# The recurrent unit's steps placed between seven-product tiles, ahead of the attention

## The reference, cut to what matters

```
h = rms_norm_2(x, g_pre) * (1 + scale) + shift
proj = h @ w_in                       # 1024 x 9216 columns
q, k, v, g_att, u, g_lru, merge = split(proj)
y_a = (dilated_attention(q, k, v) * silu(g_att)) @ w_pa
u = causal_depthwise_conv(u, conv_w, conv_b)          # 4 taps
y_b = (rg_lru(u, ...) * silu(g_lru)) @ w_pb
out = (sigmoid(merge)_a * y_a + sigmoid(merge)_b * y_b) @ w_o

rg_lru: r, i = sigmoid(block-diagonal products of u with w_rg, w_ig + biases)
        a = exp(-8 r softplus(-lambda));  h_t = a_t h_(t-1) + sqrt(1 - a_t^2) (i_t u_t)
```

## Time and profile before

| | |
|---|---|
| median of three runs | 2789.05 us |
| the profiled execution | 2786.48 us, of which its span is 2784.7 us |
| PE busy | 2733.2 us, 98% of the span |
| DVE, ACT, POOL busy | 2000.1, 1558.0, 301.9 us |
| stretch of the 18 sets | 1753.67 to 2096.48 us from the span's start |
| stretch of the recurrent unit | 2344.88 to about 2533 us |

### The profile page before, as it was taken

The page is one execution under the profiler, slowest core; times in us unless marked ns, Lnnn a source line. Parts: engine busy times, 40 slices in busy tenths (PEclk is TensorE's granted clock), DMA queues, the critical chain, the costliest instruction groups (busy, mean ns, idle before and its releaser), DMA issues.

```text
span 2784.7 us, 33128 instructions
## 1 busy us (share of the span) xinstructions
PE 2733.2 (98%) x13148; PEld 2280.7 (82%) x13148; DVE 2000.1 (72%) x2300; ACT 1558.0 (56%) x1724; POOL 301.9 (11%) x179
## 2 busy tenths in 40 slices
PE   8999999969999999999999998999999999999999
PEld 7888788858888888888888887888888888888887
DVE  7554457778888888888888888755555565666664
ACT  5322322247777777777777776322335666997122
POOL 0211000020000000000000001332321111112000
PEclk9999999989999999999999999999999999999999
DMA  6222248689999999999999964243333443114442
GB/s 198 95 75 65 87 153 291 247 344 375 385 385 386 387 386 386 386 384 390 384 386 384 386 228 164 95 121 111 101 121 134 129 122 102 49 48 144 169 149 91
DMA packets 181546, 628.30 MB, mean 226 GB/s; under 512 B 43920, under 2 KB 78096, under 8 KB 125840
## 3 DMA queue, kind: packets, MB, share of 16 engines
q1 hardware_dynamic: 176496, 609.46, 58.8%
q0 software_dynamic: 4464, 16.25, 2.2%
q10 hardware_dynamic: 432, 0.47, 0.1%
HBM read 557.74 MB, written 67.21 MB: 224 GB/s over the span
## 4 chain that ended last, share of the span: by engine, by line
PE 95%; DVE 3%; ACT 1%; DMA 1%; issue 0%; SPq 0%; DVEq 0%; ACTq 0%
PE bank L468 25%; PE bank L470 25%; PE bank L469 25%; PE bank L1894 13%; PE bank L476 3%; PE bank L2801 1%; PE bank L485 1%; PE bank L1443 1%; PE bank L794 1%; PE bank L3299 0%; DVE r_sc L1677 0%; DVE r_at L1678 0%; DVE r_best L1674 0%; PE bank L2802 0%; PE bank L854 0%
## 5 line engine op out<-in xcount | busy, mean ns | idle before, releaser
L1842 DVE TENSOR_TENSOR e_wl<-e_raw,e_wh 128x2048 fp32r<-128x2048 f32 x381 | 870.8, 2291 | 123.9 <-ACT e_wh L1834 123.5
L1834 ACT ACTIVATE e_wh<-e_raw 128x2048 fp32r<-128x2048 f32 x384 | 735.7, 1919 | 184.4 <-PE bank L470 101.0
L468 PE MATMUL bank<-e_wh,e_xh 128*128 128x512 f32 x1020 | 403.4, 395 | 0.0
L470 PE MATMUL bank<-e_wh,e_xl 128*128 128x512 f32 x1020 | 398.1, 390 | 0.0
L469 PE MATMUL bank<-e_wl,e_xh 128*128 128x512 f32 x1020 | 396.9, 389 | 0.0
L470 PEld LDWEIGHTS bank<-e_wh,e_xl 128*128 128x128 f32 x1020 | 191.4, 188 | 41.0
L469 PEld LDWEIGHTS bank<-e_wl,e_xh 128*128 128x128 f32 x1020 | 191.8, 188 | 38.1
L468 PEld LDWEIGHTS bank<-e_wh,e_xh 128*128 128x128 f32 x1020 | 191.6, 188 | 38.0 <-DVE e_wl L1842 0.4
L1894 PE MATMUL bank<-e_wh,e_hh 128*128 128x512 f32 x512 | 159.1, 392 | 0.0
L1894 PE MATMUL bank<-e_wl,e_hh 128*128 128x512 f32 x512 | 157.8, 389 | 0.0
L1894 PE MATMUL bank<-e_wh,e_hl 128*128 128x512 f32 x512 | 157.8, 389 | 0.0
(11 more groups left out here) (579 smaller groups left out, 5864.3 us busy)
## 6 DMA issues: line engine op xcount, KB each, us to landing
e_raw<-in_e_gate_dram SPq DMA_DIRECT2D x128, 1024.0 KB, 7.2
e_raw<-in_e_up_dram SPq DMA_DIRECT2D x128, 1024.0 KB, 7.5
e_raw<-in_e_down_dram SPq DMA_DIRECT2D x128, 1024.0 KB, 7.7
b_raw<-in_w_sets_dram SPq DMA_DIRECT2D x18, 1024.0 KB, 5.3
a_raw<-in_w_dram SPq DMA_DIRECT2D x12, 1024.0 KB, 5.7
a_mod_w<-in_w_mod_dram SPq DMA_DIRECT2D x48, 256.0 KB, 4.7
b_raw<-in_w_dram SPq DMA_DIRECT2D x11, 1024.0 KB, 4.9
a_x<-in_x_dram SPq DMA_DIRECT2D x16, 512.0 KB, 4.5
```

The source lines that it names most:

```text
L468: e.matmul(out, a[0], b[0], start=first, stop=False)
L470: return e.matmul(out, a[1], b[0], start=False, stop=last)
L1834: e.activation(t.e_wh[s][:, 0:2048], t.e_raw[slot][:, 0:2048], ACT.Copy).then_inc(*e.inc("e_round", i))
L1842: e.tensor_tensor(t.e_wl[s][:, 0:2048], t.e_raw[slot][:, 0:2048], t.e_wh[s][:, 0:2048].bitcast(F32), ALU.subtract).then_inc(*e.inc("e_spli ...
```

## The change

The two projections of the recurrent unit become the first eight of now 25 sets. To make room, one set of merge gates (the sixth) goes back to plain units, and these take the place of the four recurrent units among the attention. The two projections of each channel tile are stored in DRAM (`scr_lru_in`). The arithmetic of the recurrent unit is cut into steps that stand inside the loop over q. Channel tile ct has 21 products, beginning at q = 9 + 21 ct; step k stands in turn q = 9 + 21 ct + k. So step 0 stands at i = 2 of a set, and ct 6 has its steps 5 to 15 in merge-gate sets, ct 7 all its steps. The results are stored in DRAM and loaded again after the attention.

The space for this is taken from two places. The ring of parts shrinks from eight pairs to six, and AHEAD from 6 to 4. And the rows of `b_hid` for depth blocks 0 to 3 and tokens 512 to 1023, which no set uses, are stored in DRAM ahead of the sets (2 x 1 MB), their place holds the crossed sums `b_m2`, and they are loaded again at the end of the last set, ahead of the second unit of the attention.

```diff
-N_SETS = 18
+N_SETS = 25
-AHEAD = 6
+AHEAD = 4
+N_RING = 6
+LRU_FROM, LRU_EVERY, LRU_GATES = 9, 21, 6
+def lru_step(q):
+    ct, k = divmod(q - LRU_FROM, LRU_EVERY)
+    return (ct, k) if 0 <= ct < 8 else (-1, 0)
 def set_bank(g, i):
-    return (7 * g + i) % 8
+    q = 7 * g + i
+    return (q + 4 * gates_ahead(q)) % 8
 def pe_set(e, t, g):
...
+        if lru_step(q)[1] == LRU_GATES:
+            pe_lru_gates(e, t, lru_step(q)[0])
 def act_second(e, t):     # the loop over q; DVE's and SP's likewise
         act_set(e, t, *divmod(q, 7))
+        act_lru_step(e, t, *lru_step(q))
+def act_lru_step(e, t, ct, step):
+    if step == 0:   # waits l_u_in
+        e.activation(t.l_cv, t.l_u, ACT.Identity, ...)
+    if step == 3:   # waits conv_made; the gate weights are rounded too
+        e.activation(t.l_cvs[0], t.l_cv, ACT.Copy)
+    if step in (8, 9):   # half = step - 8, twice (k = 0, 1); waits lru_gate
+        e.activation(rt[own, tok], t.bank[b][own, :], ACT.Sigmoid, ...)
+        e.activation(it[own, tok], t.bank[b][other, :], ACT.Sigmoid, ...)
+    if step == 10:
+        ... Exp, Tanh, Square
+    if step == 12:  # waits lru_q, then l_gl_in
+        e.activation(tt, tt, ACT.Sqrt, ...)
+        e.activation(t.l_u, t.l_u, ACT.Silu)
+def dve_lru_step(e, t, ct, step):
+    if step in (0, 1):   # two and one taps of the convolution, 128x1024
+    if step == 4:        # low parts of l_cv and of the gate weights: lru_parts
+    if step == 11:       # waits lru_th, lru_sq: lru_q, then it * l_cv
+    if step == 13:       # waits lru_root: it * tt, then the scan
+    if step == 14:       # waits gl_made: rt * l_u: lru_made
+def sp_lru_step(e, t, ct, step):
+    if step == 2:   # waits conv_made: load of scr_lru_in[ct, 1]
+    if step == 10:  # gate weights of ct + 2
+    if step == 15:  # waits lru_made(ct): store scr_lru[ct], load scr_lru_in[ct + 1, 0]
 def sp_second(e, t):
+    e.wait_ge(*e.at("b_hid", 1, 3))
+    for part in range(2):
+        e.dma_start(t.scr_b21[part], t.b_hid[part][:, 0:4, 512:1024]...)
...
         sp_set(e, t, g, i)
+        sp_lru_step(e, t, *lru_step(q))
+        if q == 7 * (N_SETS - 1) + 3:
+            e.wait_ge(*e.at("part_spent", q))
+            for part in range(2):
+                e.dma_start(t.b_hid[part][:, 0:4, 512:1024]..., t.scr_b21[part])
 def pe_lru(e, t):
-    for ct in range(8):
-        ... seven plain tiles of 96 matmuls, and the gates
+    ... the last of four plain merge units, then the two merge tiles as before
 def sp_lru(e, t):
+    for kk in range(8):
+        e.dma_start(t.lru[:, kk, :], t.scr_lru[kk])
```

More of the change, by code:

```diff
@@ L1221, in dve_first @@
             dve_s5_inputs(e, t, b)
+        if slot == 12:
+            dve_decay(e, t)
         if slot % 8 == 6:
@@ L2326, with gates_ahead, gate_bank @@
 SET_DONE = {1: (1,), 5: (5, 2), 6: (6,)}
+LRU_FROM, LRU_EVERY, LRU_GATES = 9, 21, 6
+def lru_step(q):
+    ct, k = divmod(q - LRU_FROM, LRU_EVERY)
+    return (ct, k) if 0 <= ct < 8 else (-1, 0)
+def gates_ahead(q):
+    return sum(1 for ct in range(8) if LRU_FROM + LRU_EVERY * ct + LRU_GATES < q)
 def set_bank(g, i):
-    return (7 * g + i) % 8
+    q = 7 * g + i
+    return (q + 4 * gates_ahead(q)) % 8
+def gate_bank(ct, half, k):
+    return (LRU_FROM + LRU_EVERY * ct + LRU_GATES + 1 + 4 * ct + 2 * half + k) % 8
 def set_quarters(t, g):
@@ L2429, in pe_set @@
         for kk in range(4):
-            m = three(e, t.bank[b][:, :], [a[:, kk, :] for a in t.part_w[q % 8]], [a[:, kk, :] for a in x],
+            m = three(e, t.bank[b][:, :], [a[:, kk, :] for a in t.part_w[q % N_RING]], [a[:, kk, :] for a in x],
                       kk == 0, kk == 3)
@@ L2817, in unit @@
             which, half = u[1:]
-            pe_channels(e, t, unit_bank(u), wt, whole, t.b_hid, half, 8, ("lru_in", 0, which, half), behind=behind)
+            pe_channels(e, t, unit_bank(u), wt, whole, t.b_hid, half, 8, ("merge", 2 * which + half - 4), behind=behind)
         if unit_half_done(u):
@@ L3158, in early @@
                     t.v_y[n][:, :]).then_inc(*e.dma(f"v_out{n}", n, half))
-    for half in range(2):
-        for n in range(4):
-            early(n, half)
+    for n in range(4):
+        early(n, 0)
+    e.wait_ge(*e.at("b_hid", 1, 3))
+    for part in range(2):
+        e.dma_start(t.scr_b21[part], t.b_hid[part][:, 0:4, 512:1024].bitcast(F32)).then_inc(*e.dma(f"hid_out{part}"))
+    for n in range(4):
+        early(n, 1)
     sp_load_set(e, t, 1)
+    sp_load_lru_gates(e, t, 0)
+    sp_load_lru_gates(e, t, 1)
     for q in range(N_PARTS):
@@ L3316, in act_lru_gates @@
             e.activation(it[own, tok], t.bank[b][other, :], ACT.Sigmoid,
-                         bias=t.p["b_ig"][other, ct:ct + 1]).then_inc(*e.evict(b, "lru_gate_made", ct, half, k))
-    e.wait_ge(*e.at("decay_made"))
-    then(e).activation(at[:, :], rt[:, :], ACT.Exp, scale=t.decay[:, ct:ct + 1]).then_inc(*e.inc("lru_a", ct))
-    e.wait_ge(*e.at("lru_a", ct))
-    e.activation(rt[:, :], rt[:, :], ACT.Tanh, scale=t.decay[:, ct:ct + 1]).then_inc(*e.inc("lru_th", ct))
-    e.activation(tt[:, :], at[:, :], ACT.Square).then_inc(*e.inc("lru_sq", ct))
@@ new lines, in act_lru_step @@
+    if step == 10:
+        e.wait_ge(*e.at("decay_made"))
+        then(e).activation(at[:, :], rt[:, :], ACT.Exp, scale=t.decay[:, ct:ct + 1]).then_inc(*e.inc("lru_a", ct))
+        e.wait_ge(*e.at("lru_a", ct))
+        e.activation(rt[:, :], rt[:, :], ACT.Tanh, scale=t.decay[:, ct:ct + 1]).then_inc(*e.inc("lru_th", ct))
+        e.activation(tt[:, :], at[:, :], ACT.Square).then_inc(*e.inc("lru_sq", ct))
+    if step == 12:
+        e.wait_ge(*e.at("lru_q", ct))
+        e.activation(tt[:, :], tt[:, :], ACT.Sqrt, scale=-1.0, bias=t.k["tiny"]).then_inc(*e.inc("lru_root", ct))
+        e.wait_ge(*e.at("l_gl_in", ct))
+        e.activation(t.l_u[:, :], t.l_u[:, :], ACT.Silu).then_inc(*e.inc("gl_made", ct))
@@ new lines, in sp_load_lru_gates, with lru_part_stored, sp_load_lru @@
+def sp_load_lru_gates(e, t, ct):
+    if ct < 8:
+        if ct >= 2:
+            e.wait_ge(*e.at("lru_parts", ct - 2))
+        e.dma_start(t.l_wg[ct % 2][:, :], t.ins["w_lru"][ct]).then_inc(*e.dma(f"l_wg_in{ct % 2}", ct))
+def lru_part_stored(e, ct, which):
+    for k, w, half in SET_OUT.values():
+        if w == which:
+            e.wait_ge(*e.at(f"set_out{2 * k + ct % 2}", ct))
+def sp_load_lru(e, t, ct):
+    if ct < 8:
+        lru_part_stored(e, ct, 0)
+        e.wait_ge(*(e.at("lru_made", ct - 1) if ct else e.at("w_spent", 1)))
+        e.dma_start(t.l_u[:, :], t.scr_lru_in[ct, 0]).then_inc(*e.dma("l_u_in", ct))
@@ L3360, in pe_lru @@
 def pe_lru(e, t):
[L3361 to L3378 removed]
+    e.wait_ge(*e.at("half_split", N_HALVES - 1))
+    pe_channels(e, t, 3, t.h_w[HALF_SLOT[N_HALVES - 1]], slice(0, 128), t.b_hid, 1, 8, ("merge", -1))
+    e.mark("half_spent", N_HALVES - 1)
     for slot in range(N_MERGES):
```

302 lines of the change are left out of this document (130 added, 172 removed).

## The result

The changed kernel takes 2803.62 us in the median of five runs (2801.75 to 2808.5). Its ratio to the kernel before is 1.0057, with a 95% interval of 1.0042 to 1.0071: slower by 0.6%, about what was forecast. The forecast was 2804.4 us.

What follows compares the result with a forecast made beforehand. PE was taken as the bound (chain 95% PE). -19.0 - 0.9 + 33.2 + 2.0 = +15.3 us brings the span to 2800.0, the execution to 2801.8 and the median to 2804.4; 8 in 10 range 2777 to 2816, forecast's own 2796 to 2813.

Steps and rivals of the forecast that it cites:

- 84 matmuls fewer, wait for `b_wl`: On PE: 84 matmuls at 0.227 us save 19.0 us, and the one wait for `b_wl` goes, 0.9.
- ct 0 to 5, at parts 18 and 19: PE stalls 2.3 us at low part 18 and 0.4 at 19; 2.8 a period, 16.8 in all.
- ct 6 and 7: Channel tiles among merge sets: added sigmoids and table loads make PE stall 16.4 us together, bounds 4 and 25.
- parked rows: Behind the sets, PE's second unit waits 2 us (0 to 4) for rows SP reloads behind its wait for ct 7.
- start of the sets: Reordered start, with sums and low parts before the first products take their 11 us; costed at nothing, bound 4.
- wait for a sigmoid result behind the attention: Eight `scr_lru` loads stand on SP's queue ahead of sigmoid results wanted later; costed at nothing, bound 3.
- The alternation of DVE and POOL: A DVE operation with two SBUF inputs and a POOL operation exclude each other; sets' stalls 33.2 us by this rule.
- the walk: Timed account of one period of 21 products; low part 18 done at 59.1 us, wanted by PE at 56.8.
- a period: The 21 products of one channel tile, clock 0 where PE starts a set's first product; 2.8 us stall each.
- only merge sets stall: Rival, chance 0.17: in ct 0 to 5 the lead of 10.9 us is enough; stalls 8 us, time 2779.
- Milder delays: Rival, chance 0.17: POOL's sums fall into DVE's pauses or both run at half speed; stalls 17 us, time 2788.
- Late raw weights: Rival, chance 0.13, at `sp_load_set`: landing in 6.0 us or more delays POOL; stalls 46 to 54, time 2817 to 2825.

Runs made afterwards that it cites:

- e4: The changed kernel with each of POOL's sums in the sets replaced by two fills that read nothing; 2782.2 us in one run.
- e2: The changed kernel with the five merge-gate sets spread to sets 9, 12, 15, 18, 21 (steps 12 to 18); 2792.6 us, ratio to before 1.0016.
- e3: The changed kernel with the five merge-gate sets at 10, 13, 16, 19, 22 (steps -2 to 4); 2804.4 us in one run.
- e8: e6 plus raw weights loaded early, ACT's Silu one step later and sigmoid results stored ahead of the `scr_lru` loads; 2769.9 us, ratio to before 0.9936.
- e6: e2 with SP's reload of the parked rows issued ahead of its wait for the last channel tile's product; 2784.5 us, ratio to before 0.9985.
- e9: The changed kernel with one edit, ACT's Silu and its table load in step 13 instead of 12; 2789.9 us, ratio to before 1.0007.
- e10: e6 with ACT's Silu in step 13, raw weights and store order as in the changed kernel; 2772.4 us, ratio to before 0.9946.
- e5: The changed kernel with raw weights loaded early, at i = 3 of the set two before; 2798.8 us in one run.

## Why the prediction came out

The total was within a microsecond because errors of opposite sign cancelled, and that is luck. PE's waits in the sets were 22.9 us, where the forecast had 33.2 and a range of 25 to 42; the clock, of which it had nothing, made up most of the difference. Its steps one by one, in us of span:

| step | predicted | measured |
|---|---|---|
| 84 matmuls fewer, wait for `b_wl` | -19.9 | -19.9 |
| ct 0 to 5, at parts 18 and 19 | 16.8 | 7.95 |
| ct 6 and 7 | 16.4 | 15.0 |
| slow clock and pace in the sets | 0 | 7.1 |
| parked rows | 2.0 | 1.9 |
| start of the sets | 0 | 1.9 |
| wait for a sigmoid result behind the attention | 0 | 1.4 |
| sum (the spans differ by 15.2) | +15.3 | +15.3 |

- **Matmuls**: right. 84 went, and each product still takes 2.72 us.
- **The alternation of DVE and POOL**: right, shown twice. Operations end where the rule says, and with the sums' reads taken away DVE's operations are short again and 22.9 - 8.1 = 14.8 us of waits go (e4). The rival of half speed falls: in ct 1 POOL's first sum kept its 1.29 us though DVE's product began in its middle. The place in ct 7 the walk had not seen: there it is POOL's subtraction for a plain unit, worth 2.1 us.
- **ct 0 to 5, 2.8 us a period**: the place right, the size twice too large. On the walk's own clock, which starts at 1835.55 for ct 1, POOL's first sum began at 49.8 where the walk had 51.0, since low part 17 and the weights were there sooner. That is 1.2 us. The turns behind it (product, sum, scan, sum, low part) took 6.0 us in place of the walk's 6.8, since each was a little shorter than the operation alone: 0.8 more. So low part 18 was done at 57.1 and not at 59.1. PE wanted it at 56.3. The walk's 56.8 was a slip of 0.5 the other way, for its own rule gives 20 x 2.72 + 1.75 + 0.2 = 56.35. With the rule the walk would have had a wait of 2.75, and the 2.0 us of error leave 0.8. Where a wait is a small difference of long chains, its size needs a range of its own; the one given (0 to 4) held it.
- **ct 6 and 7**: the sum right (16.4 against 15.0), the reason half wrong. I priced the added table loads and sigmoids as work. e2 and e3 show that the tie matters: a sigmoid of a bank just made holds ACT at PE's pace, and all that stands behind it starts with no lead. In ct 7's end no POOL operation held up the scan, which took 2.29, and of PE's wait of 4.1 only 2.1 were the alternation at the low part behind it. How much of the 15.0 is the tie and how much that the merge sets stand back to back is not shown.
- **The clock**: the step that was missing. Behind the three waits of about 4 us in the sets the granted clock was 0.53 to 0.64 for 3 to 5 us. e8, which has no waits, needs 491.5 us for the sets, so about 5.6 of the 7.1 us go with the waits: 4.7 of it is the clock, the rest the matmuls just behind a wait.
- **Parked rows**: right in place and size. SP's wait for the last channel tile held them back (e6), as the walk had it.
- **Start**: 1.5 of 1.9 us is the slow stretch at 1725, which comes and goes from run to run: from 1725 to 1740 the clock was 1.00 in e6 and e8, and 0.89 in e9 and e10, with the same work there.
- **Sigmoid result**: costed at nothing because of SP's queue; it is ACT's own wait for the stores of the heads. The bound of 3 held.
- **Rivals**: "only merge sets stall" is out, since PE waited in all of ct 0 to 5. "Milder delays" as half speed is out by the first sum of ct 1; in size the truth lay between the two, with 22.9 us of waits against its 17 and the forecast's 33.2. "Late raw weights" as priced (46 to 54 us of stalls) did not come, but the weights landed in 5.6 us in the median instead of 5.3, and e5 shows 3.2 us of waits that hang on them.
- **A reading that was not whole**: the earlier trace rows shows two of PE's waits from 2040 us on. There are more, the largest 1.7 us for `t_s` and 1.1 for `o_l`; both are the same after the change, so the sum does not suffer.

What the prediction did not see is how near the change was to paying. One step of ACT in another turn is worth 13.7 us (e9 against the changed kernel). With the merge sets and the reload moved as well the kernel takes 2772.4 us (e10), and 2769.9 with all edits (e8), which is what a cover of all the unit's work was priced at (2769).

## What to carry to other kernels

When work of other engines is put between the parts that PE needs in order, don't sum its busy time: find for each engine the turn at which it loses its lead, put long functions behind the part that is rounded there and not ahead of it, and keep operations on what PE has just made, which tie their engine to PE, from standing ahead of a long stretch. Contention between DVE and POOL need not be removed if it can be moved to where parts are still ahead.

## What the runs showed of the hardware

A POOL operation that only writes (a fill) does not delay DVE operations with two SBUF inputs: product, scan and low part took 1.23, 2.29 and 0.67 us beside fills, and 1.82, 3.26 and 1.71 beside sums. A longer POOL operation that reads costs more: beside a subtraction of 1024 columns a low part of 0.68 us took 2.77. And one and the same wait of 2.38 us at 1725 left the clock at 1.00 in one execution and at 0.51 for 3.2 us in another, so 1.5 us of difference there says nothing of a kernel.
